# Attention units on one core: scores two units ahead, maxima in front of the combination, adaLN products by half a block at the head of the unit

## The reference

```python
logits = einsum('bqhmd,bkhmd->bmhqk', q, k) * scale + bias      # differential, m = 0, 1
p = softmax(logits);  a = p[:, 0] - lam * p[:, 1];  out = einsum('bhqk,bkhe->bqhe', a, v)
...
ml = split(silu(c) @ w_ada[i] + b_ada[i], 6)                    # adaLN
```

## Time and profile before

| what | value |
|---|---|
| median of three runs | 2234.18 us (2228.84 to 2234.39) |
| the profiled execution, own time | 2224.44 us |
| its span, first to last instruction | 2221.9 us |
| mean granted TensorE clock over the span | 0.932 |
| PE busy, PEld, DVE, ACT, POOL | 90%, 74%, 52%, 39%, 12% |
| HBM read | 257.92 MB |

### The profile page before, as it was taken

How to read it: one execution, slowest core, us unless ns; L and a number is a source line. 1 busy time by engine, 2 the same in 40 slices (tenths; PEclk the granted TensorE clock), 3 DMA queues, 4 the chain that set the end, 5 groups by cost and what they waited for, 6 DMA issues and landing times. The chain is left out here.

```text
span 2221.9 us, 36714 instructions
## 1 busy us (share of the span) xinstructions
PE 2000.3 (90%) x15607; PEld 1649.1 (74%) x15607; DVE 1146.2 (52%) x1799; ACT 877.5 (39%) x1560; POOL 256.6 (12%) x292
## 2 busy tenths in 40 slices
PE   5987999898899999888899969889999979788998
PEld 4746998774699888655688846768888768567986
DVE  4555675554577554333755564544444545435643
ACT  4344554434465543343322232422222344445542
POOL 1100121110022100001311151120000021001000
PEclk9988999998799999986799979999999989998999
DMA  7564665456366432341000021332322214004653
GB/s 241 170 247 131 173 188 187 152 191 242 111 186 184 170 116 84 114 152 48 6 4 4 3 77 57 83 93 94 93 94 95 95 36 134 21 1 133 190 174 129
DMA packets 230936, 261.34 MB, mean 118 GB/s; under 512 B 14070, under 2 KB 153590, under 8 KB 230647
## 3 DMA queue, kind: packets, MB, share of 16 engines
q1 hardware_dynamic: 221351, 256.06, 35.9%
q10 hardware_dynamic: 9424, 2.95, 0.7%
HBM read 257.92 MB, written 1.07 MB: 117 GB/s over the span
## 5 line engine op out<-in xcount | busy, mean ns | idle before, releaser
L399 PE MATMUL acc<-rounded,rounded 128*128 128x512 f32 (+1 forms) x2552 | 881.4, 345 | 35.0 <-DVE rounded L643 11.2
L400 PE MATMUL acc<-rounded,rounded 128*128 128x512 f32 (+1 forms) x2552 | 876.1, 343 | 0.0
L401 PE MATMUL acc<-rounded,rounded 128*128 128x512 f32 (+1 forms) x2552 | 876.0, 343 | 0.0
L383 DVE TENSOR_TENSOR rounded<-arena,rounded 128x2048 fp32r<-128x2048 f32 x194 | 435.3, 2248 | 321.3 <-ACT rounded L372 321.2
L399 PEld LDWEIGHTS acc<-rounded,rounded 128*128 128x128 f32 x2552 | 489.5, 192 | 102.3 <-issue 27.0
L400 PEld LDWEIGHTS acc<-rounded,rounded 128*128 128x128 f32 x2552 | 489.3, 192 | 60.0 <-issue 0.5
L401 PEld LDWEIGHTS acc<-rounded,rounded 128*128 128x128 f32 x2552 | 488.4, 191 | 60.7
L372 ACT ACTIVATE rounded<-arena 128x2048 fp32r<-128x2048 f32 x194 | 362.9, 1873 | 364.1 <-PE acc L401 341.9
L809 PEld LDWEIGHTS sc<-arena 128*128 128x128 f32 x592 | 78.3, 208 | 74.4 <-ACT arena L912 70.1
L809 PE MATMUL sc<-arena 128*128 128x64 f32 (+1 forms) x592 | 88.3, 300 | 44.4 <-ACT arena L912 42.7
L897 ACT ACTIVATE arena<-acc,stat 128x256 f32<-128x256 f32 (+2 forms) x128 | 66.3, 522 | 108.8 <-DVE stat L839 78.2
(11 more groups left out here) (242 smaller groups left out, 1839.0 us busy)
## 6 DMA issues: line engine op xcount, KB each, us to landing
arena<-in_w_ff SPq DMA_DIRECT2D x64, 1024.0 KB, 5.2
arena<-in_w_ada SPq DMA_DIRECT2D x48, 1024.0 KB, 5.1
arena<-in_w_up SPq DMA_DIRECT2D x88, 512.0 KB, 5.0
arena<-in_w_in SPq DMA_DIRECT2D x24, 1024.0 KB, 5.1
arena<-in_w_down SPq DMA_DIRECT2D x20, 1024.0 KB, 5.0
arena<-in_w_out SPq DMA_DIRECT2D x16, 1024.0 KB, 5.5
arena<-in_w_in_even SPq DMA_DIRECT2D x9, 1024.0 KB, 5.2
arena<-in_w_in_odd SPq DMA_DIRECT2D x8, 1024.0 KB, 5.1
```

The lines of the kernel that those rows point to most:

```text
L383: dve.tensor_tensor(r32(w), w, r32(high_slot(c)[:, 0:size(c)]), ALU.subtract).then_inc(split_made, 1)
L399: pe.matmul(ps, ah, bh, start=first, stop=False)
L400: pe.matmul(ps, ah, bl, start=False, stop=False)
L401: return pe.matmul(ps, al, bh, start=False, stop=last)
```

## The change

- PE computes the scores of two units before the first step, and scores(u+2) in step u.
- The adaLN product is cut in its two weight chunks: the first in step 2i, the second in step 2i+1, each at the head of the step, before the scores. The bank is claimed with the first.
- DVE does maxima(u) before combine(u-1).
- The turn of the adaLN block stays between values(u-1) and turn(u) in even steps. No instruction is added or taken away.

```diff
             def tensor(self, pe):
                 self.scores(pe, 0)
+                self.scores(pe, 1)
                 for u in range(self.n):
-                    if u + 1 < self.n:
-                        self.scores(pe, u + 1)
+                    if self.ada:
+                        ada_pe(pe, self, u // 2, u % 2)
+                    if u + 2 < self.n:
+                        self.scores(pe, u + 2)
                     if u >= 1:
                         self.values(pe, u - 1)
-                    if self.ada and u % 2 == 0:
-                        if u:
-                            ada_turn(pe, self, u // 2 - 1)
-                        ada_pe(pe, self, u // 2)
+                    if self.ada and u and u % 2 == 0:
+                        ada_turn(pe, self, u // 2 - 1)
                     self.turn(pe, u)
...
             def vector(self, dve, hook=None):
                 for u in range(self.n + 2):
+                    if u < self.n:
+                        self.maxima(dve, u)
                     if 1 <= u <= self.n:
                         self.combine(dve, u - 1)
-                    if u < self.n:
-                        self.maxima(dve, u)
...
-        def ada_pe(pe, att, i):
+        def ada_pe(pe, att, i, n):
 
-            b = att.ada[i]
-            if b == 0:
+            b, f = att.ada[i], att.ada_fill(i)
+            if b == 0 and n == 0:
                 pe.wait_ge(silu_ready, 1)
-            ps = claim(pe, "sc", att.ada_fill(i))
-            for n in range(2):
-                g = ada_chunk[b] + n
-                wait_landed(pe, g)
-                w = shaped(raw_slot(g), g)
-                for k in range(4):
-                    rows = slice(k * QUARTER, (k + 1) * QUARTER)
-                    ins = pe.matmul(ps[rows, :], silu_c[:, 4 * n + k, :], w[:, k, :], start=(n == 0), stop=(n == 1),
-                                    tile_position=(0, k * QUARTER))
-                ins.then_inc(sc_full if n else chunk_read, 1)
+            ps = bank("sc", f) if n else claim(pe, "sc", f)
+            g = ada_chunk[b] + n
+            wait_landed(pe, g)
+            w = shaped(raw_slot(g), g)
+            for k in range(4):
+                rows = slice(k * QUARTER, (k + 1) * QUARTER)
+                ins = pe.matmul(ps[rows, :], silu_c[:, 4 * n + k, :], w[:, k, :], start=(n == 0), stop=(n == 1),
+                                tile_position=(0, k * QUARTER))
+            ins.then_inc(sc_full if n else chunk_read, 1)
```

## The result

The changed kernel takes 2167.32 us, median of four runs (2164.3 to 2172.52), beside 2231.51 us for the kernel before in the same session (2227.52 to 2234.39): a ratio of 0.972 with a 95% interval of 0.970 to 0.974, or 64 us less. The forecast was 46 us less; the time lies at the low edge of the range. The profiled execution of the changed kernel took 2172.52 us against 2224.44 before, 52 us less. The number of instructions is the same, 36714.

A forecast was written before the change was run, and what follows sets the result against it. PE, busy 90% of the span, was taken as the bound, so only its waits and low clock could give time: 26.5 us idle plus 20 us clock, say 46, off the median gives 2188 us; range 2167 to 2214.

The forecast's parts named there:

- only work together: DVE's maxima before the combination and scores two ahead: each was said to need the other; no separate size given.
- the walk: Step-by-step count of PE's waits in attention stages: 0.4 us for outputs at the step's head, 8.7 us idle per att1.
- The idle time: PE's waits in the six attention stages: 26.5 us saved.
- the differential pair: Pair of units in att1: falls from 6.36 to about 5.85 us, including a 0.4 us wait for outputs.
- The MoBA pair: Pair of MoBA units: 6.5 us against 7.34, since the even turn covers the bank.
- The clock: Low-clock time in the attention stages: half of 41 us extra comes back, 20 us, bounds 0 and 41.
- attD's steady part: Steady units of attD: no gain, since PE is busy 17.25 of 17.48 us.
- The clock gives nothing: Rival, attention stages: low stretches follow the gaps that stay, only idle time comes back, 2208 us; chance 0.20.
- Gives all: Rival, attention stages: all 41 us of low-clock extra come back besides the idle time, 2167 us; chance 0.10.
- New waits at the head: Rival: waiting for outputs costs 1.0 us or more in each of 24 adaLN pairs, 2230 us; chance 0.09.
- the change does not do what it says: Rival: scores(u+2) reach PE before exps(u) are done, units stay in lockstep with ACT, 2226 us; chance 0.05.
- The loads in series: Rival, adaLN weight loads: chunks move one after the other, an att1 pair takes 10.2 us, 2274 us; chance 0.06.

The follow-up runs named there:

- the spread squares: Changed kernel with att1's eight sub-norm squares done one each in steps 5 to 12 instead of all in step 11: 2152.69 us, ratio 0.965.
- all three edits: Changed kernel with adaLN half behind scores(u+2), squares one a step, and ACT's copy of the adaLN bank behind the next even exponentials: 2154.7 us, ratio 0.966.

## Why the prediction was right, and where its sizes were off

**What bounds, and what moves.** Right: only PE's idle time and its clock had time to give. DVE's order breaks the chain of maxima, exponentials and combination, and it does so only with the scores ahead (the maxima first alone gave nothing, both together 41 us). That the two "only work together" was too strong: the scores ahead gave 20 us alone, by the wait of the maxima for late scores in the wide units, which the walk did not have. The gain is in the six stages and no others.

**The idle time** was put at 26.5 us and is 33.7. The terms that were mis-sized: the differential pair, put at 5.85 us, takes 5.57, because the wait for `outputs` at the head is 0.18 and not 0.4; my walk added whole durations where PE starts the next group before the last one ends. The MoBA pair takes 6.24 and not 6.5. In att1(0) the walk's 8.7 us are 6.5: 1.7 at the start (2.0), 0.5 in the differential pairs and nothing in the MoBA pairs (2.2 together), 1.9 behind the squares (2.1), 2.4 at the end (2.4). So it is the steady pairs that were charged too much there. attBl and attBc idle 0.4 and 1.1 us (I had 1.4 and 1.9), for the half at the head covers more of their starts than I counted. attC and attD were right: 4.8 and 4.6 us against 5.3 and 4.1, with the gaps at the ends 0.84 instead of 0.75 each.

**The clock** was put at 20 us, half of what there was, and gave 22.2. The size was right; the half was a choice and not a derivation. Which gaps it depends on only the spread squares showed: behind the 1.86 us that I left standing came 11.48 us at 0.55.

**From the profile to the median.** Sum 46, the profiles say 52, the medians 64. The step that failed here is to take the 46 us off the median as they stand, as if the profiled execution lay 9.7 us under it after the change too. The profiled execution before had a high clock, 0.932, and single runs of the kernel before, beside the last group of experiments, range from 2225.39 us at 0.933 to 2239.57 at 0.924. A difference of 0.009 in the clock goes with 14 us of time there. The changed kernel's profile, at 2172.52, was the slowest of its four runs. So up to 12 of the 18 us missed lie in which execution was profiled, and 6 in the sum (10 too little in the six stages, less the 4 lost in the others). The time lies 0.3 us above the lower bound of the range, and the runs of the changed kernel scatter over 8 us: that the range held is in part luck.

**attD's steady part** was given nothing, against the rule of the Trainium skill ("Perfetto Trace Analysis", Identifying the Most-Contended Engine), by which the weight loads' busy time left room. A unit takes 3.86 us from scores to scores after the change, against 3.88 before (17.48 for 4.5 units), so for this change the row was the right guide; no run here tried another way to use that room:

```profile
1907.87 1.13 PE L790 MATMUL acc<-arena 64*128 64x512 f32 x4
...
1911.73 1.13 PE L790 MATMUL acc<-arena 64*128 64x512 f32 x4
```

**The rivals.** "The clock gives nothing" falls with 22 us. "Gives all", 2167, has the measured time but not the mechanism: 37 us at the low clock are left in these stages, and the spread squares took 14.6 us more by removing most of those in att1, with their gaps. New waits at the head are 0.18 us and not 1.0; that rival was also summed wrongly, since 24 pairs with 0.6 us more than the walk had are 14 us, or 2202 and not 2230. That the change does not do what it says falls with the scores that don't wait in the steady loop. The loads in series were tried and are not what happens here.

**What the prediction did not have:** that having half of the adaLN product in every step is a gain by itself (29 us alone, 23 on top), and that its place decides through ACT's list. I had weighed the head of the step by PE and DVE alone. So the 46 us and the 64 are not made of the same parts: of the 64, 41 come from the scores and the maxima, and 23 from the halves, whose place at the head the walk had charged with a wait.

## What to carry to other kernels

When a filler is moved in one engine's list, follow also who copies its result and what is queued behind that copy: here one scores group of delay cost 19 us through an activation that waited in front of the exponentials, and moving the copy gave it back. Cut filler work to one even piece a step, and spread a rare lump (eight squares in one step) over the steps, since PE pays for a gap twice: by its length and by the low clock behind it. Before a single profile is set against a median, compare its mean clock with those of other executions.

## What the runs showed of the hardware

The clock fell behind gaps far shorter than the 3.4 us of the forecast: a gap of 1.86 us in the changed kernel was followed by the 11.48 us at 0.55 above, and without it both att1 stages run at 0.99 to 1.00. How much low time a given gap brings differs between executions: attC, whose order is the same in both, had 7 us of it in the profile of the kernel before and 17.7 in that of the kernel with only the halves; and the two gaps at the start of att1(0), 0.62 and 0.85 us, brought 3.4 us in one profile and none in another.

The loads kept up beside a loop that asked for more of them. The Trainium skill ("DMA: Bandwidth & Descriptors", Specifications) puts HBM's share of a core at about 358 GB/s. In short stretches the trace is above that, 402 GB/s; over the steady part of att1(0) in the changed kernel it is 362 for 30.7 us, and in the kernel with all three edits 378 for 40 us. The two longer stretches, in the stretches view of each:

```profile
118.00:148.70 30.70, 28.31 (x219) 15.67 (x217) 20.21 (x76) 18.28 (x72) 0.00 (x0) 1.00 1.02 362
```

```profile
116.00:156.00 40.00, 39.21 (x311) 22.69 (x304) 27.10 (x101) 25.49 (x91) 1.64 (x1) 1.00 1.03 378
```

So here, with one core at work, the page's figure is no ceiling, neither for a burst nor as a mean over 40 us. Nor do these means measure a limit: they are the pace at which PE releases the slots of the ring. In the second stretch SP's queue waits for such a release for 34.8 of the 40 us (waits view of SP: what it waited for, us in total, times, longest):

```profile
SPq L353 <- PE sc L1090: 25.1, 11, 3.4
SPq L353 <- PE sc L809: 9.7, 3, 3.2
```

PE waits for no weight load in either stretch, though the DMA engines' share is above 1.00. A load took 5.9 us to landing in the first stretch (median of nine), against 5.0 where only one is under way, so loads that follow each other without a break do take longer; how much shorter the loop could get before PE met that, no run here shows.
